# The first norm of a float32 two-block network: dividing by the root early, and half of the conditioning slabs multiplied on TensorE

## What is computed

```python
c_act = jax.nn.silu(c)
mod = (c_act @ w_ada + b_ada)[:, None, :]
shift1, scale1, gate1, shift2, scale2, gate2 = jnp.split(mod, 6, axis=-1)
h = rms_norm(x, norm1_w) * (1.0 + scale1) + shift1
x = x + gate1 * hybrid_mixer(h, w_in, ...)       # first step: p = h @ w_in
def rms_norm(x, w):
    y = x * lax.rsqrt(jnp.mean(x * x, axis=-1, keepdims=True) + RMS_EPS)
    return y * w
```

## Time and profile before

| | |
|---|---|
| median of 3 runs | 2085.97 us (2085.11 to 2091.56) |
| the profiled execution | 2089.39 us, span of its instructions 2088.2 us, mean granted TensorE clock 0.970 |
| TensorE busy | 1940.8 us (93% of the span) |
| VectorE, ScalarE, GpSimd busy | 686.0, 710.3, 954.8 us (33%, 34%, 46%) |
| HBM traffic | 180.6 MB, 87 GB/s over the span |
| first 40 us | eight pairs of w_ada arrive at some 410 GB/s; TensorE has done its share of them at 40.3 us |

### The profile page before, as it was taken

The page is one execution under the profiler, slowest core; times in us unless marked ns, Lnnn a source line. Parts: engine busy times, 40 slices in busy tenths (PEclk is TensorE's granted clock), DMA queues, the critical chain, the costliest instruction groups (busy, mean ns, idle before and its releaser), DMA issues.

```text
span 2088.2 us, 32887 instructions
## 1 busy us (share of the span) xinstructions
PE 1940.8 (93%) x13928; PEld 1655.1 (79%) x13928; DVE 686.0 (33%) x1069; ACT 710.3 (34%) x1093; POOL 954.8 (46%) x1257
## 2 busy tenths in 40 slices
PE   5989998999999999999999899977777799999997
PEld 4667776777888889999999899966666478888885
DVE  5654454223111102332210156544554422222101
ACT  2563222332222323222222334354445432322222
POOL 3543232545545665554545465421112265555563
PEclk9999999999999999999999999988989899999998
DMA  7332231233333232223222322000000323323221
GB/s 281 123 135 87 67 104 65 81 111 121 121 91 96 91 96 91 91 92 91 89 88 88 126 91 87 31 7 2 2 2 2 131 81 103 99 91 96 90 100 58
DMA packets 54690, 182.75 MB, mean 88 GB/s; under 512 B 6512, under 2 KB 6768, under 8 KB 54416
## 3 DMA queue, kind: packets, MB, share of 16 engines
q1 hardware_dynamic: 54544, 180.65, 26.6%
HBM read 175.39 MB, written 5.24 MB: 87 GB/s over the span
## 4 chain that ended last, share of the span: by engine, by line
PE 83%; DVE 6%; ACT 4%; DMA 3%; issue 2%; POOL 1%; SPq 1%; DVEq 0%; ACTq 0%
PE PS L498 69%; PE PS L615 3%; PE PS L969 1%; DMA RAWS<-w_w_in 1%; DMA ADA<-w_ada 1%; PE PS L962 1%; POOL WL L2171 1%; PE PS L976 1%; DMA BON<-bsave 1%; PE PS L987 1%; PE PS L533 1%; DMA RAWS<-w_f0g 1%; PE PS L634 0%; DVE HL L1585 0%; PE PS L943 0%
## 5 line engine op out<-in xcount | busy, mean ns | idle before, releaser
L2171 POOL TENSOR_TENSOR WL<-RAWS,WH 128x256 fp32r<-128x256 f32 x1074 | 824.2, 798 | 780.2 <-ACT WH L1666 780.1
L498 PE MATMUL PS<-HH,WH 128*128 128x264 f32 (+2 forms) x2184 | 668.8, 348 | 42.6 <-POOL WL L2171 9.4
L498 PE MATMUL PS<-HL,WH 128*128 128x264 f32 (+2 forms) x2184 | 655.3, 342 | 0.0
L498 PE MATMUL PS<-HH,WL 128*128 128x264 f32 (+2 forms) x2184 | 653.1, 341 | 0.0
L498 PEld LDWEIGHTS PS<-HH,WH 128*128 128x128 f32 (+1 forms) x2184 | 377.7, 190 | 108.6 <-issue 22.7
L1666 ACT ACTIVATE WH<-RAWS 128x1024 fp32r<-128x1024 f32 (+2 forms) x275 | 283.7, 1033 | 475.2 <-PE PS L498 401.1
L498 PEld LDWEIGHTS PS<-HH,WL 128*128 128x128 f32 (+1 forms) x2184 | 378.4, 190 | 48.4 <-issue 0.6
L498 PEld LDWEIGHTS PS<-HL,WH 128*128 128x128 f32 (+1 forms) x2184 | 378.9, 190 | 47.7 <-issue 2.1
L498 PE MATMUL PS<-IHf,WH 128*128 128x512 f32 (+1 forms) x704 | 209.4, 338 | 0.0
L498 PE MATMUL PS<-IHf,WL 128*128 128x512 f32 (+1 forms) x704 | 209.3, 338 | 0.0
L498 PE MATMUL PS<-ILf,WH 128*128 128x512 f32 (+1 forms) x704 | 209.2, 338 | 0.0
(11 more groups left out here) (498 smaller groups left out, 1814.7 us busy)
## 6 DMA issues: line engine op xcount, KB each, us to landing
RAWS<-w_w_in SPq DMA_DIRECT2D x52, 512.0 KB, 4.4
RAWS<-w_ada SPq DMA_DIRECT2D x32, 512.0 KB, 3.6
RAWS<-w_f0g SPq DMA_DIRECT2D x22, 512.0 KB, 3.6
RAWS<-w_f0u SPq DMA_DIRECT2D x22, 512.0 KB, 3.7
RAWS<-w_f1g SPq DMA_DIRECT2D x22, 512.0 KB, 3.6
RAWS<-w_f1u SPq DMA_DIRECT2D x22, 512.0 KB, 3.5
RAWS<-w_f2g SPq DMA_DIRECT2D x22, 512.0 KB, 3.5
RAWS<-w_f2u SPq DMA_DIRECT2D x22, 512.0 KB, 3.6
```

Source lines behind the costliest of these rows:

```text
L498: ins = te.matmul(ps[0:m, q, o:o + b - a] if len(halves) > 1 else ps[0:m, o:o + b - a], w[:, k * m:k * m + m], v[:, k0 + k, a:b], start=fi ...
L2171: ins = ge.tensor_tensor(WL[s % NS][:, p], RAW[i % NR][:, p], WH[s % NS][:, p].bitcast(f32), ALU.subtract)
```

## The change

- DIRECT becomes slabs 0, 2, 4 and 6 of each part: four of eight go through TensorE, four are weighed by VectorE. The pairs are loaded in their plain order.
- `sum_squares(0)` moves between the direct products of part 0 and those of part 1.
- VectorE multiplies X by RSTD into a new tile XRS, in between its weighed slabs of part 1 and waiting for RSTD. XRS lies where ADA's follower tiles will lie, among them ST, so GpSimd's clearing of ST moves behind the last of the norm.
- Once SC is there, ScalarE makes HH straight from XRS, scale and shift in one instruction, without waiting for VectorE; VectorE makes TMP with a scale and a shift (one tensor input) and HL = TMP - HH.

```diff
+    XRS = sbuf("XRS", [128, KT * T1], st=m0)
...
-    DIRECT = (0, 1)
+    DIRECT = (0, 2, 4, 6)
...
-    ADA_PAIRS = (1, 0, 2, 3, 4, 5, 6, 7)
+    ADA_PAIRS = tuple(range(8))
...
         te.wait_ge(*c_act.at("silu"))
-        for v in range(2):
-            ada_direct(v, bank(v))
+        ada_direct(0, bank(0))
         te.wait_ge(s_k0, 16)
         sum_squares(0)
+        ada_direct(1, bank(1))
         ada_column(0, bank(0))
         ada_column(1, bank(1))
...
         ve.wait_ge(s_in, 16)
+        ve.wait_ge(s_x, 16)
         for j in WEIGHED[:16 - 2 * len(DIRECT)]:
             ve.wait_ge(s_ad[j // 2], 16)
             weigh(j, ADA[:, j, :])
+            for k in {9: (0, 1), 11: (2, 3, 4), 13: (5,), 15: (6, 7)}.get(j, ()):
+                ve.wait_ge(*n_rs.at("r0"))
+                ve.tensor_tensor(XR[k], X[:, k, NM:T2], RSTD[:, 0:T1], ALU.mult).then_inc(*n_xr.up(k))
...
-        ve.wait_ge(s_x, 16)
-        apply_norm(0, SC[:, 0:8], MOD[:, 0:8], NM)
+        def first_low(k):
+            ve.wait_ge(*n_h.at(k))
+            ve.wait_ge(*n_hi.at(k))
+            ve.tensor_tensor(HL[:, k, NM:T2], TMP[k % 3][:, 0:T1], HH[:, k, NM:T2].bitcast(f32),
+                             ALU.subtract).then_inc(*n_lo.up(k))
+
+        for k in range(KT):
+            ve.wait_ge(*n_xr.at(k))
+            if k >= 3:
+                ve.wait_ge(*n_lo.at(k - 3))
+            ve.tensor_scalar(TMP[k % 3][:, 0:T1], XR[k], SC[:, k:k + 1], MOD[:, k:k + 1], ALU.mult,
+                             ALU.add).then_inc(*n_h.up(k))
+            if k:
+                first_low(k - 1)
+        first_low(KT - 1)
...
-        upper(0, MOD[:, 0:8], NM)
+        ae.wait_ge(*s_sc.at(0))
+        for k in range(KT):
+            ae.wait_ge(*n_xr.at(k))
+            ae.activation(HH[:, k, NM:T2], XR[k], ACT.Identity, bias=MOD[:, k:k + 1],
+                          scale=SC[:, k:k + 1]).then_inc(*n_hi.up(k))
...
-        ge.memset(ST[:, :, :], 0.0).then_inc(*zeros.up("st"))
         begin("w_in", IN_ORDER[10], 1)
+        ge.wait_ge(*n_lo.at(7))
+        ge.memset(ST[:, :, :], 0.0).then_inc(*zeros.up("st"))
```

More of the change, by code:

```diff
@@ L330, in program @@
     n_res, n_pre, n_outp = count("n_res"), count("n_pre"), count("n_outp")
+    n_xr = count("n_xr")
     ff_silu, ff_mul, ff_hi, ff_lo, ff_x = (count(x) for x in ("ff_silu", "ff_mul", "ff_hi", "ff_lo", "ff_x"))
@@ L446, in place @@
         return pair((job + 2) % 3) if f == 1 else bank(job % 6)
+    XR = [XRS[:, 512 * k:512 * k + 512] for k in range(KT)]
     NORMED = {0: 0, 1: 1, 3: 2, 4: 3, 5: 4}
@@ L1049, in weigh @@
             z = WEIGHED.index(j)
-            if k == (0 if v >= 2 else len(DIRECT)):
+            if k == (0 if v >= 2 else 1):
                 if v >= 2:
@@ L1054, in weigh @@
             else:
-                ve.wait_ge(*weighed(j - 1))
+                ve.wait_ge(*ada_acc.at(z - 1))
                 ve.scalar_tensor_tensor(a[:, :], w, CA[:, k:k + 1], a[:, :], ALU.mult, ALU.add).then_inc(*ada_acc.up(z))
@@ L2197, in gpsimd @@
         ge.memset(ROW[:, :], 0.0).then_inc(*zeros.up("row"))
+        begin("w_in", IN_ORDER[10], 1)
+        ge.wait_ge(*n_lo.at(7))
         ge.memset(ST[:, :, :], 0.0).then_inc(*zeros.up("st"))
-        begin("w_in", IN_ORDER[10], 1)
         def project_rest():
```

## The result

Median of 20 executions each: before 2087.43 us, after **2094.03 us**; ratio 1.0028, 95% interval 1.0015 to 1.0042. So the change costs 6.6 us by the medians. (The ratio is not the quotient of the two medians, which would be 1.0032; further down, too, ratios and medians can differ by some hundredths of a percent, and by 0.14% in one case.) The same two kernels were measured a second time (first experiment): 2087.52 and 2096.54 us, ratio 1.0045 (1.0027 to 1.0063), 9.0 us. The forecast was +9.0 us, 2095.0 us.

The account below looks back on a forecast made before the run. TensorE was taken to set when the conditioning is ready; +9.9 on TensorE, -0.5 and -0.5 on GpSimd gave +8.9, say +9.0 us, so 2095.0 us against the median 2085.97; range 2090 to 2099.5.

Parts of the forecast that it names:

- TensorE, +9.9 us: Last column sum later: four more direct slabs +13.9 us, less 2.6 for the earlier start and 1.4 of gap.
- rival B: Sum of squares lifts TensorE's clock for a while; two or three slabs cost 1.5 us less each, 2091; chance 0.06.
- VectorE's new multiplications, zero: Eight multiplications into XRS at 0.74 us each, hidden by TensorE's direct products with 7 us of cover: zero.
- GpSimd, -0.5 and -0.5: Before WL of w_in: -0.5 us from ST's clearing leaving the path, -0.5 from less contention with VectorE.
- the bound of -1.7: Contention with VectorE in GpSimd's six WL pieces: at best none left, -1.7 us.
- Norm alone is worth zero on TensorE: Norm behind SC done some 4 us sooner, but TensorE waits for GpSimd's WL: zero.
- C: First projection stays at low clock longer: 25 more products run low, +5 us, 2100; chance 0.05.
- A: Unbroken one-column products lift TensorE's clock; a slab takes 2.0 us in place of 3.48, 2081; chance 0.06.
- D: Norm or GpSimd behind the last column sum worth more, -2.9 and -5.4 us, leaving +4.5, 2090.5; chance 0.05.
- my 6.3 us line: Whole kernel: differences up to 0.3% (6.3 us) count as no change, so 2092.2 us is the line.
- 0.82 for "slower by over 0.3%": Whole kernel: chance 0.82 of slower, above 2092.2 us; same had 0.15, faster 0.03.

Follow-up runs that it names:

- direct_only: Kernel before with four direct slabs of eight, plain load order and moved sum of squares, but old norm and clearing of ST: 2097.03 us, 1.0046.
- early_low_after: Changed kernel, but GpSimd makes its six WL pieces before it waits for the last column sum: 2092.15 us, 1.0031 to the kernel before.
- again: The changed kernel, unedited, measured a second time: 2096.54 us, 1.0045 to the kernel before.
- early_low_again: Second measurement of the kernel before with GpSimd's six WL pieces made before the wait for the last column sum: 2084.42 us, 1.0007.
- pool_after_sc: Changed kernel, but GpSimd starts WL only when SC is done: 2094.33 us, 1.0047 to the kernel before.
- long_memset: Changed kernel with one existing GpSimd clearing (the second STG) made 515 columns wide: 2091.16 us, 1.0029 to the kernel before.
- early_low_before: Kernel before, but GpSimd makes its six WL pieces before it waits for the last column sum: 2081.28 us, 0.9975.
- norm_only: Changed kernel with direct slabs 0 and 1 and the old load order, sum of squares still between the direct parts: 2085.38 us, 0.9989 to the kernel before.

## Why the prediction was right in size, and where it was wrong

- **TensorE, +9.9 us: right.** 13.79 and 13.65 us for the two parts against 13.9 each. The last column sum, forecast at 50.25, ended at 50.0 in direct_only, 50.54 in early_low_after and 50.91 in again, with the first pair 0.2 to 1.1 us later than the forecast had it. In the first execution it ended at 47.48.
- **That exception is rival B**, the burst of clock behind the sum of squares, to which I gave 0.06. It was there in the first profile: 62 records in 10 us, where again has 49. These are the windows of after and, below it, of again:

```profile
30.50:40.50 10.00, 10.00 (x62) 10.00 (x63) 8.49 (x11) 2.85 (x4) 0.00 (x0) 0.66 0.40 156
```

```profile
30.50:40.50 10.00, 10.00 (x49) 10.00 (x48) 8.43 (x11) 3.00 (x4) 0.00 (x0) 1.00 0.43 167
```

  The clock column misleads here: it reads 1.00 in again, whose records keep the slow pace, because in that execution no change of the clock is recorded before 60 us, and the column reads 1.00 until the first one. So this stretch is read by the pace of its records. Of 11 executions with the sum of squares between the direct parts, 5 showed the burst and 6 did not, again among these 6 with the very same code. The 0.06 was far too low. "It has never been seen after this sum before" was too strong from one profile: early_low_again has the old order and shows it too, in TensorE's timeline: its 32 records of column sums took 3.83 us, not 6.83.

```profile
34.17 3.83 PE L533 MATMUL PS<-KC,ACC 128*128 128x1 f32 x32
```

- **VectorE's new multiplications, zero: right.** They took 0.62 to 0.68 us each against the 0.74 forecast. The last XRS ended at 40.22 (forecast 40.9), 7.3 us before MOD. RSTD was ready at 31.7 (forecast 31.1; the start had come 0.8 late), and the wait before XRS was 7.17 (forecast some 7).
- **GpSimd, -0.5 and -0.5: wrong**, and this is the step that failed. Removing ST's clearing was priced at its own duration, and contention at an average price per piece. Both took the way in which the engines share for given. It flipped: WL fell from 1.065 to 0.69 a piece, which by itself is *more* than forecast (-2.3 against -0.5) and more than the bound of -1.7, but VectorE was held for those 4.5 us and became the one waited for. HL now releases TensorE where WL had. Net +0.35 in place of -1.0, shown by pool_after_sc, long_memset and early_low_after to come from how WL's pieces meet the norm. Where the engines do alternate, in long_memset, the price of contention was about right: 5.77 us for six pieces against 6.39, -0.6 for the -0.5. The bound was wrong for another reason: 0.775 a piece was taken as the price of GpSimd alone, but VectorE was at work beside the first of those four pieces. The kernel before has four at 0.69 a little later:

```profile
61.40 2.77 POOL L2171 TENSOR_TENSOR WL<-RAWS,WH 128x256 fp32r<-128x256 f32 x4 [3.54 <-ACT WH L1666]
```

- **"Norm alone is worth zero on TensorE": right in result** (0.9989), for another reason than given. It did not wait longer for WL; it waited for HL.
- **C** did not happen: the projection stayed low for 9 products (7 in again), not for more. In before it was 15. From w_in's first product to the last of the pair that makes 11.24 and 10.91 us in place of 12.63, so 1.4 to 1.7 us came back that the forecast had not counted. Nothing shows this to be an effect of the change: over the 14 profiles the number runs from 7 to 15, with 13 in direct_only and 15 in long_memset. (The pause of 2.38 us in before is not what made it long: early_low_before has none, and 14 such products.) **A** did not happen: in again TensorE worked without a pause from 13.24 to 50.91, in one-column products but for the sum of squares, and they kept their pace of 0.2133 to 0.2175 us a record. **D** did not happen, and early_low_after shows that it could not have paid for the slabs.
- **The sum.** 9.9 + 0.35 - 1.5 (the shorter low stretch) = 8.75; the forecast had 9.9 - 1.0 = 8.9. Two misses of over one us cancelled, and that is luck. Measured +6.6 and +9.0. Both medians lie inside the range. A burst as in B takes 3.1 us off this sum, so a mix of executions with and without it would lie between 5.65 and 8.75 (an estimate: only one execution of each kernel has a profile). That the change is slower is clear, that it is slower by over 0.3% is not: by its median the first measurement lies 0.3 us over my 6.3 us line, by its ratio, 1.0028, under it, with an interval from 1.0015 to 1.0042. So 0.82 for "slower by over 0.3%" was more certainty than a measurement of this spread can bear out.

The Trainium skill (SBUF — State Buffer, section "SBUF: two separate sides") has VectorE and GpSimd share one port pair as an exclusive lock, which whichever starts first keeps for its whole instruction while the other blocks. The runs agree in kind: one engine works and the other stands still. But here one VectorE instruction was held over six of GpSimd's in a row in four executions (after, again, norm_only, pool_after_sc), and over one at a time in others. The rule by itself gives only the second. What decides between the two is open: SC is recorded as begun at 47.72, 0.38 us *before* the first piece, so the records don't show who asked first.

## What to carry to other kernels

Price work by the engine that ends last. Four slabs cost VectorE 1.3 us each, and it had 6.6 us to spare; on TensorE, which had 1.4, they cost 3.5 each. Of these 14 us only the earlier start and the filled gap (2.6 and 1.4 forecast) came back, and 9.7 us were left at the last column sum (direct_only), whatever else the change improves.

Before removing a small instruction that "only" clears a buffer, look at what runs behind it and beside which engine. Here its 0.5 us kept two engines in step. Moving the reading work behind it into GpSimd's idle stretch before the column sum took the wait for it away, though it slowed VectorE's work there and no median shows a gain for sure.

Don't read a change of 0.3% off two profiles. Compare the stretch that was edited in several of them, and leave the end to the median.

## What was not expected of the hardware

- A VectorE instruction of 128 by 8 elements can be held 4.52 us by six GpSimd pieces of 0.69 us (after, again, norm_only), or the instruction behind it 4.59 us, where it takes 0.54 (pool_after_sc). An instruction of the same size that reads PSUM was not held (0.17 us, early_low_before). With 0.42 us more of clearing in front (long_memset), the same two streams alternated at 0.96 and 0.90 us.
- The same kernel, executed again, had its one-column products at 10.55 or at 13.65 us for 64, with the same products and no pause ahead of them; the first pair landed at different times as well, from 12.33 to 13.24 us in the kernels with that load order.
- The granted clock between 200 and 460 us, in unchanged code, differed by 27 us of low time between two executions, worth 9.2 us: as much as the whole change.
